# Router fold five slots later, the first tile's logits ahead of the second tile's additions, and the branch register loaded by each engine on its own

## What is computed

```python
x = x + g1 * hybrid_mixer(h, w_in[l], w_out[l], ...)     # h = rms_norm(x) * (1 + sc1) + sh1
h = rms_norm(x, norm_ffn_g[l]) * (1.0 + sc2) + sh2
f = moe_ffn(h, router_w[l // 2], moe_w_gate[l // 2], moe_w_up[l // 2], moe_w_down[l // 2])
...
def moe_ffn(h, w_router, w_gate, w_up, w_down):
    logits = xf @ w_router                                # 256 tokens, 8 experts
    top_logits, top_idx = lax.top_k(logits, TOP_K)        # 2 experts a token
    top_w = softmax(top_logits)
    ...                                                   # each expert: swiglu(x, w_gate[e], w_up[e], w_down[e]), weighted
```

## Time and profile before

| | |
|---|---|
| median of 3 runs | 2445.71 us |
| lowest and highest | 2440.72 and 2449.26 us |
| the profiled execution, its own time | 2445.38 us |
| its span in the trace | 2444.1 us |
| mean granted PE clock | 0.967 of full |
| busy: PE, PEld, DVE, ACT | 2310.9, 1894.0, 1706.2, 1412.8 us |
| chain that ended last | PE 85%, DVE 7%, ACT 5%, issue 2% |

### The profile page before, as it was taken

How to read it: one execution, slowest core, us unless ns; L and a number is a source line. 1 busy time by engine, 2 the same in 40 slices (tenths; PEclk the granted TensorE clock), 3 DMA queues, 4 the chain that set the end, 5 groups by cost and what they waited for, 6 DMA issues and landing times.

```text
span 2444.1 us, 34902 instructions
## 1 busy us (share of the span) xinstructions
PE 2310.9 (95%) x10627; PEld 1894.0 (77%) x10627; DVE 1706.2 (70%) x2214; ACT 1412.8 (58%) x2063; POOL 42.2 (2%) x69
## 2 busy tenths in 40 slices
PE   6999999897999999999999799988999999879998
PEld 5777887676788888888888678877888788668887
DVE  4777877665899998998999755466554555654554
ACT  4545444444777777778777654456544544575443
POOL 1000111000000000000000000000000000000000
PEclk8999999998999999999999989999999999889999
DMA  8755886643899999999999945543556465321661
GB/s 296 274 168 178 303 297 240 235 150 91 291 367 353 348 367 354 357 359 352 367 352 367 314 138 183 193 157 111 174 185 192 158 195 180 124 73 61 207 189 52
DMA packets 411195, 571.46 MB, mean 234 GB/s; under 512 B 28103, under 2 KB 324465, under 8 KB 410962
## 3 DMA queue, kind: packets, MB, share of 16 engines
q1 hardware_dynamic: 401200, 543.13, 66.8%
q0 software_dynamic: 6960, 23.79, 3.1%
q10 hardware_dynamic: 2930, 3.22, 0.4%
HBM read 568.98 MB, written 1.05 MB: 233 GB/s over the span
## 4 chain that ended last, share of the span: by engine, by line
PE 85%; DVE 7%; ACT 5%; issue 2%; DMA 1%; SPq 1%; ACTq 0%; DVEq 0%
PE bank L344 75%; DVE lo L323 2%; PE bank L537 1%; PE bank L2499 1%; ACT xn L102 1%; ACT hi L321 1%; PE bank L2606 1%; SPq L270 1%; DVE xn L102 1%; PE bank L772 1%; DVE x_res L102 1%; ACT L102 1%; DVE small L102 1%; DMA router_sb<-router_w 1%; ACT aT_hi L102 1%
## 5 line engine op out<-in xcount | busy, mean ns | idle before, releaser
L323 DVE TENSOR_TENSOR lo<-raw,hi 128x1024 fp32r<-128x1024 f32 x997 | 1178.0, 1221 | 191.1 <-ACT hi L321 176.5
L321 ACT ACTIVATE hi<-raw 128x1024 fp32r<-128x1024 f32 x997 | 1004.5, 1054 | 121.5 <-PE bank L344 110.1
L344 PE MATMUL bank<-hi,aT_hi 128*128 128x512 f32 (+1 forms) x2016 | 816.5, 405 | 28.2 <-ACT proj L102 11.6
L344 PE MATMUL bank<-hi,aT_lo 128*128 128x512 f32 (+1 forms) x2016 | 793.0, 393 | 0.0
L344 PE MATMUL bank<-lo,aT_hi 128*128 128x512 f32 (+1 forms) x2016 | 792.3, 393 | 0.0
L344 PEld LDWEIGHTS bank<-hi,aT_hi 128*128 128x128 f32 x2016 | 385.0, 191 | 110.0 <-issue 17.7
L344 PEld LDWEIGHTS bank<-hi,aT_lo 128*128 128x128 f32 x2016 | 384.4, 191 | 82.5 <-issue 0.4
L344 PEld LDWEIGHTS bank<-lo,aT_hi 128*128 128x128 f32 x2016 | 385.9, 191 | 75.0 <-issue 1.7
L344 PE MATMUL bank<-hi,hidT_hi 128*128 128x512 f32 x792 | 310.6, 392 | 6.6 <-DVE hidT_lo L547 5.7
L344 PE MATMUL bank<-lo,hidT_hi 128*128 128x512 f32 x792 | 309.3, 391 | 0.0
L344 PE MATMUL bank<-hi,hidT_lo 128*128 128x512 f32 x792 | 309.3, 390 | 0.0
(11 more groups left out here) (305 smaller groups left out, 1605.0 us busy)
## 6 DMA issues: line engine op xcount, KB each, us to landing
raw<-moe_w_gate SPq DMA_DIRECT2D x352, 256.0 KB
raw<-moe_w_up SPq DMA_DIRECT2D x352, 256.0 KB
raw<-moe_w_down SPq DMA_DIRECT2D x176, 512.0 KB
raw<-ffn_w_gu SPq DMA_DIRECT2D x352, 256.0 KB
raw<-ffn_w_down SPq DMA_DIRECT2D x110, 512.0 KB
raw<-ada_w SPq DMA_DIRECT2D x56, 512.0 KB
raw<-w_in SPq DMA_DIRECT2D x56, 512.0 KB
ada_slot<-ada_w POOLq DMA_DIRECT2D x40, 512.0 KB, 6.0
```

Source lines behind the costliest of these rows:

```text
L321: act.activation(hi[u % SPL][:, :], raw[r % RAW][:, :], ACTF.Copy).then_inc(hi_done, 1)
L323: dve.tensor_tensor(lo[u % SPL][:, :], raw[r % RAW][:, :], hi[u % SPL][:, :].bitcast(F32), ALU.subtract).then_inc(lo_done, 1)
L344: ins = pe.matmul(bank, left[a], right[b], start=first and n == 0, stop=last and n == 2)
```

## The change

`fold_router` moves from slot 6 to slot 10, and its matmul and copy become `fold_bias` at slot 11. In layer 1 `out_second` no longer splits three units ahead. In `rest` both halves of tile 0's logits come first, then the two additions of tile 1 with their transposes, and both splits ahead of the second `best`. `busiest_i` is made inside `choose`; PE loads its register ahead of the gather, ACT and DVE behind the expert weights, without the check of the value's bounds.

```diff
-    def out_second(left, marks, between=lambda: None, gate=None, inside=lambda i: None):
+    def out_second(left, marks, between=lambda: None, gate=None, inside=lambda i: None, ahead=3):
...
-        split_to(u + 7)
+        split_to(u + 4 + ahead)
...
         b = DVE.run([b], dve.reduce_sum, rows_of_b, prod.rearrange("p (k e) -> p e k", k=KD), axis=AX.X)
+        route.update(folded=[a], rows_of_b=(rows_of_b, b))
+
+    def fold_bias():
+
+        rows_of_b, b = route["rows_of_b"]
         PE.need(b, *bank_mark[7])
         m = PE.did(pe.matmul(psum[7][:, 0:NE], ones_sq[:, :], rows_of_b, start=True, stop=True))
         m = DVE.run([m], dve.tensor_copy, router_b[:, :], psum[7][:, 0:NE])
         bank_mark[7] = (m,)
-        route["folded"] = [a, m]
+        route["folded"].append(m)
...
-            if n == 6 and layer:
+            if n == 10 and layer:
                 fold_router()
+            if n == 11 and layer:
+                fold_bias()
...
-        out_second([a[:, 4:8, :] for a in aT], chain["T"], between, 0, inside)
+        out_second([a[:, 4:8, :] for a in aT], chain["T"], between, 0, inside, 0 if layer else 3)
...
-        def score(t):
-            PE.need(*xT_marks[t, 0], *xT_marks[t, 1], *route["folded"])
-            for k in range(KD):
+        def score(t, half):
+            PE.need(*xT_marks[t, half], *route["folded"], *(() if half else bank_mark[2 + t]))
+            for k in range(4 * half, 4 * half + 4):
...
+            n = DVE.run([n], dve.tensor_copy, busiest_i[:, :], busiest[:, :])
             return eq4, w4, by_tile[2], n
...
-        def rest():
+        def rest(most):
+            score(0, 0)
+            score(0, 1)
             run_late(1)
             turn(1, 0)
-            score(0)
+            run_late(1)
+            turn(1, 1)
+            score(1, 0)
             split(0)
-            run_late()
-            turn(1, 1)
+            rstd(1)
             best(0)
-            rstd(1)
-            score(1)
-            split_hi = split
+            score(1, 1)
+            split(1)
             b = best(1)
-            eq4, w4, out, n = choose([b])
-            split_hi(1)
+            split_to(st["use"] + 1)
+            eq4, w4, out, busy = choose([b])
+            PE.need(busy)
+            pe.reg_load(most[mybir.EngineType.PE], busiest_i[0:1, 0:1])
             first_pair()
-            busy = DVE.run([n], dve.tensor_copy, busiest_i[:, :], busiest[:, :])
             route["weights"] = weights(eq4, w4, out)
             route["r"] = r
-            return busy
+            ACT.need(busy)
+            act.reg_load(most[mybir.EngineType.Activation], busiest_i[0:1, 0:1])
+            DVE.need(busy)
+            dve.reg_load(most[mybir.EngineType.DVE], busiest_i[0:1, 0:1])
...
-        busy = route["rest"]()
+        most = nc.alloc_registers("busiest", compute)
+        route["rest"](most)
         PE.need(*(m for b in range(4) for m in bank_mark[b]))
-        for e in (PE, ACT, DVE):
-            e.need(busy)
...
-        most = nc.values_load(busiest_i[0:1, 0:1], engines=compute, min_val=0, max_val=S)
...
-        with nc.If(most > SLOTS):
+        with nc.If_cmp(most, SLOTS, "IS_GT"):
```

More of the change, by code:

```diff
@@ L2197, in split @@
                                in1=xn_split[0][:, t, :].bitcast(F32), op0=ALU.mult, op1=ALU.subtract)
-        def score(t):
-            PE.need(*xT_marks[t, 0], *xT_marks[t, 1], *route["folded"])
-            for k in range(KD):
+        def score(t, half):
+            PE.need(*xT_marks[t, half], *route["folded"], *(() if half else bank_mark[2 + t]))
+            for k in range(4 * half, 4 * half + 4):
                 ins = pe.matmul(psum[2 + t][:, 0:NE], hT_full[:, k, t * P:(t + 1) * P], router_g[:, k, :], start=k == 0, stop=k == KD - 1)
-            logits[t] = PE.did(ins)
+            if half:
+                logits[t] = PE.did(ins)
         def best(t):
```

## The result

The changed kernel takes 2422.81 us (median of 4 runs, 2420.34 to 2428.22) against 2443.22 for the kernel before on the same chip: 20.4 us less. The ratio of the runs is 0.9923, interval 0.9903 to 0.9942. The forecast was 2426.5 with a range of 2420 to 2434. So the time agrees with the forecast to some 4 us in one measurement and 8 in the other, and how well the prediction did has to be read from the stretches.

What follows compares the result with a forecast made beforehand. PE, busy 95% of the span, was taken to stand still at the router's fold and in routing up to the second expert step. 2445.38 - 9.9 (fold) - 9.0 (routing and branch) = 2426.5 us, range 2420 to 2434.

Steps and rivals of the forecast that it cites:

- The fold, 9.9 us: Router's fold in the mixer: moving it saves PE's stall (7.98) and low clock (2.17), less its matmul (0.22).
- a small load in a full queue: Reason given for the fold's stall: the router's 32 KB load took 13.8 us with the DMA engines' share at 1.09.
- The gather, 6.2 us earlier: Routing, from the last mixer matmul: the gather starts at 595.1 instead of 601.35.
- The jump under the gather: Branch to the experts: PE's sequencer runs ahead, so its 3.4 us jump lies largely under the 6.57 us gather.
- A jump worth only 0.1 us: Alternative price for PE's branch: hiding it gains nothing, this part gives 6.2 and 0.6, and the estimate is 2428.7.
- DVE's `lo` is late next: Second expert step: DVE's first split after the branch is done at 611.1, and PE waits 3.5 us for it.
- The clock, 2.9 us in the second step: Second expert step: after PE's idle time the low clock returns, 24 matmuls taking 8.38 instead of 5.47 us.
- Routing and branch, 9.0 us: From routing through the second expert step: that step ends at 622.4 instead of 631.47.
- Rival 2: Second expert step: the clock stays high or comes back sooner, another 2.9 us, 2423.6; chance 0.13.
- Rival 3: Experts: the stream of expert weights sets the pace, so their end follows its start, 2429.3; chance 0.12.
- Rival 6: Whole kernel: slower, as a mean granted clock lower by 0.01 would lose 23 us, 2449.6; chance 0.03.
- Rival 4: Routing gives nothing, as DVE's and ACT's jumps are fetched while SP's loads run; only the fold counts, 2435.5; chance 0.07.

Runs made afterwards that it cites:

- fold_only: The kernel before with only the fold moved, in two parts at slots 10 and 11; ratio 0.9958 to the kernel before.
- router_first: The changed kernel with the fold back at slot 6 and the router's load issued ahead of the gate loads; 2426.08 us, ratio 0.9928 to the kernel before.
- splits_ahead: The changed kernel with DVE's splits ahead of tile 1's additions again, as in the kernel before; ratio 0.9919 to the kernel before.
- turn_first: The changed kernel with tile 0's logits behind tile 1's additions and transposes on PE; ratio 0.9912 to the kernel before.
- cast_late: The changed kernel with the cast of `busiest_i` and PE's register load behind all DVE work on the gathered tokens; ratio 0.9934 to the kernel before.
- load_behind: The changed kernel with PE's register load behind the gather's matmuls instead of ahead of them; ratio 0.9924 to the kernel before.
- after_again: The changed kernel measured a second time without an edit; 2418.24 us against 2442.42 for the kernel before, ratio 0.9895.
- weights_ahead: The changed kernel with the expert weights worked out beside the gather, ahead of ACT's and DVE's registers and jumps; ratio 0.9913 to the kernel before.
- fold_back: The changed kernel with the fold back at slot 6; ratio 0.9953 to the kernel before.
- two_more: The changed kernel with two more weight units split ahead of the branch (six instead of four) and two fewer behind; ratio 0.9934 to the kernel before.

## Why the prediction was right, point by point

- **The fold, 9.9 us**: 9.95 in the first profile, 9.92 in fold_only. Stall, low clock and cover were as worked out. The fold's matmul cost 0.14 and not 0.22. The reason given for the load's 13.8 us ("a small load in a full queue") was about half of it, as router_first shows: ahead of the gate loads it took 6.9. What is left of the stall there, 2.8 us, is DVE's own queue.
- **The gather, 6.2 us earlier**: 6.83. The path was as walked. That tile 0's logits at their new place take 2.0 us was too much: the transposes began 1.54 us after PE's last mixer matmul ended, and this is most of the 0.6 by which the gather came sooner than forecast. The two timelines divide the 6.83: 2.0 up to the first transposes of tile 1 (1.54 us instead of 3.54), 3.8 from there to the second `best` (6.80 instead of 10.61; before, the second addition stood behind `xn_lo` of tile 0, and ACT waited 1.74 us for it), and 1.0 behind it, where the other `xn_lo` has left. By experiment, splits_ahead gives 2.5 to the splits and turn_first 0.26 to the logits; the remaining 4 us are read from the timelines alone. The splits did not hold `x_pair`: DVE waited 0.47 us for PE in front of it.
- **The jump under the gather**: the mechanism was right (begun 2.6 us before the gather's end), its price wrong. The prediction had the jump at 3.4 and the first step 7.0 us after the gather's start. The jump takes 4.3 to 5.75 there, since its instruction transfer starts late beside the loads that the same order of splits sets off, and the first step came at 7.66 and 8.62. It changed little, because the step after it waits for DVE anyway, as the sum assumed. A jump worth only 0.1 us, which the prediction set aside, would not fit: cast_late put the jump back behind the gather and lost 5.3 us at the first step. That the register is loaded ahead of the gather was not needed, as load_behind shows; the integer has to be ready.
- **DVE's `lo` is late next**: right. Predicted ready 16.0 us after the gather's start, PE went on at 16.15. The wait was 1.87 instead of 3.5, as the first step came later and had a gap of 0.72. In after_again it was 0.08, as the first step ran at the low clock. weights_ahead removes it.
- **The clock, 2.9 us in the second step**: mis-sized. From the start of the second step to that of the third it took 10.14 against 8.43, 1.7 more. The clock was low for 3.4 us of it; before, it was low for 10.2 us, which took in most of the first step. In the kernel after the first step kept the high clock after 1.88 us of idle time, in after_again it had the low one after 2.33. The sum also puts the wait for `hid` at nothing. With the high clock that wait alone makes the step 9.5 us, so of the 1.7 the clock adds only 0.6 to what the wait would have cost.
- **Routing and branch, 9.0 us**: 10.66, and 11.5 in after_again. The error in the first, 1.7, is the gather's 0.6 and the clock's 1.2, less 0.15 by which the second step began late.
- **Rival 2** (the clock stays high in the second step, 2423.6) is nearer to both measured times than the forecast, but not for its reason: where the clock did stay high, the wait for `hid` took its place. **Rival 3** (the weights' stream sets the pace) is refuted for this stretch: from the third step to the transposes of the last expert step (1384.95 before, 1358.80 after) it took 753.48 and 753.50 us. **Rival 6**: the mean clock rose, from 0.967 to 0.970 and 0.973. **Rival 4**, its cause (a jump fetched while loads run), is real on PE; its effect was not.

The parts sum to 9.9 + 10.7 = 20.6 us beside 20.4 measured, and in the repeat to 9.9 + 11.5 = 21.4 beside 24.2. The closeness of the first pair is luck in part: unedited code varies by more than that. None of the variants beats the changed kernel measurably: the best stretch, weights_ahead's, is 1.5 to 2.3 us shorter, and its interval overlaps with both measurements of the changed kernel.

## What to carry to other kernels

Move a small preparation behind work that does not need it, and look first at what stands ahead of its load in its own queue. A far jump costs a fetch (3.4 us here for the whole jump, up to 5.7 beside bulk loads): have the value that it tests early, and keep bulk loads out of the microseconds around the branch. When a stall on one engine goes, check the second wait behind it before counting the whole gain: here 5.3 us at the first step were 2.9 at the third, and behind the wait for `lo` stood one for `hid`.

## What was not expected of the hardware

- A taken far jump of PE holds one 16 KB instruction transfer and takes 3.37 to 3.57 us on PE with DMA shares of 0.03 to 0.19 during it, and 4.31 to 5.75 with shares of 0.58 to 0.96. The Trainium skill's "Runtime: NRT & Kernel Launch", Instruction fetch mechanics, has the fetch by DMA; this trace agrees, and adds that it can start up to 3.4 us after the branch beside bulk loads, against 1.0 to 1.2 without.
- On ACT and DVE the branch's own record is 54 and 56 ns, yet ACT's next instruction came 2.5 us later in the kernel after and DVE's 3.8 (2.8 to 3.1 in before, load_behind, fold_back and cast_late), though nothing that the trace names was late. The traces do hold an instruction transfer of 8 KB that starts 0.9 to 1.2 us after ACT's branch and one 1.0 to 1.3 us after DVE's in twelve of them, without naming the engine that it is for. In two_more, where they start 2.1 and 1.6 us after, the next instruction comes 3.9 us after the branch on both. I read the gap as the jump's cost there; no run tests it.
- The same code at the same place ran the stretch from L1353 to the last mixer matmul in 38.98 to 39.01 us in seven of the profiles and in 40.24 to 41.61 in the other six, and the last 1815 us varied by 9 us. Both go with the granted clock. In the first stretch it was 0.50 over six us of the kernel before and 1.00 at the same place of the kernel after. For the second, the windows of 120 us at 1564.95 before and 1538.80 after, which lie equally far behind the experts' end:

```profile
1564.95:1684.95 120.00, 106.47 (x483) 84.50 (x482) 78.26 (x132) 72.14 (x127) 0.00 (x0) 0.97 0.44 142
```
```profile
1538.80:1658.80 120.00, 107.81 (x462) 85.15 (x461) 75.72 (x129) 69.63 (x123) 0.00 (x0) 0.91 0.43 137
```

The third column from the right is the granted clock, 0.97 and 0.91. What decides it where the code is the same was not found.
